# A decoder layer on one core: the expert weight ring with a third slot for six passes only, six embedding products inside the expert passes, x1 kept in DRAM

## The reference

```python
h = rms_norm(x, g_mix); proj = h @ w_in            # conv value | conv gate | q | k | v
conv_out = conformer_conv(c_val, c_gate, ...)      # GLU, causal depthwise conv of 31, LayerNorm, silu
attn = moba_attention(rope(q), rope(k), v)         # 8 heads x 64, blocks of 256, top-3 past blocks + own
x = x + concat(rms_norm(conv_out), rms_norm(attn)) @ w_out          # this x is "x1"
x = x + hier_moe(rms_norm(x, g_ffn), ...)          # top-1 of 4 groups, then top-2 of 8 SwiGLU experts
gate = sigmoid(rms_norm(x, g_ple) @ w_ple_gate + b_ple_gate)
x = x + (p @ w_ple_proj) * gate                    # p: 256 numbers per token, "embedding product"
out = rms_norm(x, g_final)
```

## Time and profile before

| | us |
|---|---|
| median of 3 runs | 597.26 |
| lowest, highest | 595.72, 597.45 |
| the profiled execution's own time | 595.68 |
| its span | 593.8 |

### The profile page before, as it was taken

How to read it: one execution, slowest core, us unless ns; L and a number is a source line. 1 busy time by engine, 2 the same in 40 slices (tenths; PEclk the granted TensorE clock), 3 DMA queues, 4 the chain that set the end, 5 groups by cost and what they waited for, 6 DMA issues and landing times.

```text
span 593.8 us, 8744 instructions
## 1 busy us (share of the span) xinstructions
PE 506.3 (85%) x3193; PEld 299.7 (50%) x3193; DVE 295.0 (50%) x559; ACT 185.4 (31%) x355; POOL 77.9 (13%) x91
## 2 busy tenths in 40 slices
PE   1899999998879989945999989787777988899994
PEld 1688888775556668842433323222222332237883
DVE  2509989999996955484122121101111111167676
ACT  4832320325785352512011010000000000056655
POOL 0570000000032040010211111111110111000000
PEclk9999999999799989975999998888899888999998
DMA  8920400444505050594699999999999899748003
GB/s 336 387 77 2 146 11 8 155 155 161 216 1 214 1 214 35 187 415 167 257 416 421 417 419 422 418 411 419 400 396 420 357 395 413 313 185 331 1 1 141
DMA packets 34741, 146.10 MB, mean 246 GB/s; under 512 B 5776, under 2 KB 6032, under 8 KB 22928
## 3 DMA queue, kind: packets, MB, share of 16 engines
q1 hardware_dynamic: 28800, 133.72, 56.6%
q0 software_dynamic: 5328, 10.50, 4.7%
q10 hardware_dynamic: 576, 1.37, 0.6%
HBM read 140.85 MB, written 12.58 MB: 258 GB/s over the span
## 4 chain that ended last, share of the span: by engine, by line
PE 50%; SPq 20%; DMA 12%; DVE 8%; ACT 5%; issue 4%; POOL 1%; DVEq 0%; POOLq 0%; ACTq 0%
PE bank L1466 15%; SPq L563 9%; DMA wring<-w_up_in 8%; PE bank L1706 8%; PE bank L1770 7%; PE bank L1566 5%; SPq L570 4%; SPq L496 4%; PE bank L1490 4%; DMA wring<-w_in_in 2%; PE bank L1726 2%; PE bank L1749 2%; DMA arena<-rows_d,tfirst 1%; PE bank L1607 1%; DVE wring L1072 1%
## 5 line engine op out<-in xcount | busy, mean ns | idle before, releaser
L1706 PE MATMUL bank<-wring,arena 128*32 128x512 f32 x704 | 90.0, 670 | 20.3 <-DMA wring<-w_up_in 18.0
L1010 DVE SCALAR_TENSOR_TENSOR mix<-arena,pr,mix 128x512 f32<-128x512 f32 x120 | 86.6, 790 | 0.0
L1362 DVE TENSOR_TENSOR arena<-arena,bank 128x256 f32<-128x256 f32 x16 | 6.7, 421 | 141.7 <-ACT arena L898 141.7
L1706 PEld LDWEIGHTS bank<-wring,arena 128*32 128x32 f32 x704 | 27.5, 121 | 81.7 <-issue 76.9
L898 ACT ACTIVATE arena<-bank 128x256 f32<-128x256 f32 x16 | 6.2, 384 | 145.1 <-PE bank L1706 145.1
L1706 PE MATMUL bank<-mix,arena 128*32 128x512 f32 x240 | 40.4, 663 | 7.9 <-DMA arena<-w_up_in 7.9
L1726 PE MATMUL bank<-wring,arena 128*32 128x512 f32 x352 | 40.0, 595 | 5.3 <-ACT arena L901 5.3
L1706 PE MATMUL bank<-arena 128*32 128x512 f32 x80 | 40.3, 663 | 0.0
L1367 DVE COPY arena<-bank 128x512 f32<-128x512 f32 x16 | 11.1, 692 | 53.4 <-PE bank L1726 53.4
L1466 PE MATMUL bank<-hT_hi,win_hi 128*128 128x512 f32 x128 | 33.5, 398 | 1.9 <-DVE hT_lo L988 1.3
L1466 PE MATMUL bank<-hT_lo,win_hi 128*128 128x512 f32 x128 | 31.6, 389 | 0.0
(11 more groups left out here) (258 smaller groups left out, 901.4 us busy)
## 6 DMA issues: line engine op xcount, KB each, us to landing
wring<-w_gate_in SPq DMA_DIRECT2D x22, 1024.0 KB, 15.5
wring<-w_up_in SPq DMA_DIRECT2D x22, 1024.0 KB, 18.8
wring<-w_down_in SPq DMA_DIRECT2D x22, 1024.0 KB, 20.8
wring<-w_in_in SPq DMA_DIRECT2D x5, 2048.0 KB, 19.3
arena<-w_down_in SPq DMA_DIRECT2D x5, 1024.0 KB, 11.6
mix<-w_gate_in SPq DMA_DIRECT2D x5, 1024.0 KB, 15.1
mix<-w_up_in SPq DMA_DIRECT2D x5, 1024.0 KB, 17.2
arena<-w_gate_in SPq DMA_DIRECT2D x5, 1024.0 KB, 19.2
```

The lines of the kernel that those rows point to most:

```text
L1010: ins = dve.scalar_tensor_tensor(out=mixc[:, mm, :], in0=u[:, mm, j:j + S], scalar=w, in1=mixc[:, mm, :], op0=ALU.mult, op1=ALU.add)
L1706: ins = pe.matmul(pb[2 + s][lo:hi, :], xgT[:, s, k, lo:hi], up_w(w, a)[:, :, k, :], start=(k == 0), stop=(k == DK - 1))
```

## The change

1. *Start.* SP issues the constant tables and the router weights, behind the four chunks of w_in. ACT issues only the identity (64 KB) and the parameters. eps is set by a DVE memset, and ACT runs one square root on it first. PE waits for the identity; the waits for the tables move to their first uses.
2. *Ring.* Slot 2 is used by passes 2 and 5 only. Passes 6 to 15 alternate between slots 0 and 1, so the last pass is in slot 1. `last` is n - 3 up to pass 7 and n - 2 from pass 8. Between the reloads of passes 7 and 8 SP loads w_pp and pT into the arena, once pass 5 is done.
3. *x1.* SP stores `xs` tile by tile to a DRAM tensor `x1_d` after the output projection, and reads it back behind the weights of pass 15. In between, `xs` holds the gate and up weights of pass 3, a = 0 (2.1 MB), issued ahead of the passes.
4. *Rows first.* The up DMAs of pass 2, a = 1, and all that SP issues behind them, wait until the first two gathers have landed.
5. *Embedding products.* Six of the eight stand at the head of passes 8 to 13, in banks 4 and 5, each with its copy on ACT. Two stay in the tail.
6. *Tail.* w_pg's first half goes to slot 0 once pass 14 is done; bias and final gain are issued right behind it instead of behind the y tiles and the second half. The y tiles go to slot 1. DVE adds one y tile at a time between the splits.

The same addresses move with slots 0 and 1 (`wpg`, `yg`, `x2_lo` and the rest). The core of the diff:

```diff
+THREE = 2 * SLOTS
+MADE = 8
...
-            return n % SLOTS if n < STRAIGHT else (STRAIGHT % SLOTS, (STRAIGHT + 1) % SLOTS)[n % 2]
+            return n % SLOTS if n < THREE else n % 2
...
+        def load_of(n):
+            return n // SLOTS + 1 if n < THREE else n // 2
+        def aside(n, a):
+            return isinstance(n, int) and n == SLOTS and a == 0
+        def up_aside():
+            return xs[:].rearrange("p t n -> p (t n)").rearrange("p (w k n) -> p w k n", w=2, k=DK)
...
@@ sync
+            sp.dma_start(c[:, P:C_MASK], cst[:, P:C_MASK]).then_inc(const_loaded, 16)
+            sp.dma_start(c[:, C_MASK:C_END], cst[:, C_MASK:C_END]).then_inc(const_loaded, 16)
+            sp.dma_start(wr[:], w_r.rearrange("(p k) n -> p k n", k=DK)).then_inc(wr_loaded, 16)
...
+            for t in range(TT - 1):
+                for half in range(2):
+                    banks.wait_emptied(sp, ("outc", 2 * t + half))
+                sp.dma_start(x1_rows[:, t], xs[:, t, :]).then_inc(x1_stored, 16)
             banks.wait_full(sp, ("outc", 2 * TT - 1))
             load_up(1, 1, 1)
             for a in range(2):
                 load_down(1, 1, a)
-            for a in range(2):
-                load_up(2, 2, a)
+            for half in range(2):
+                banks.wait_emptied(sp, ("outc", 2 * TT - 2 + half))
+            sp.dma_start(x1_rows[:, TT - 1], xs[:, TT - 1, :]).then_inc(x1_stored, 16)
+            load_up(2, 2, 0)
+            for s in range(2):
+                sp.wait_ge(gathered[s], 16)
+            load_up(2, 2, 1)
...
+            for i, src in enumerate((w_gate, w_up)):
+                sp.dma_start(up_aside()[:, i],
+                             src[bass.ds(expert(SLOTS, 0), 1)].rearrange("e (p k) n -> p (e k) n", k=DK)
+                             ).then_inc(aside_loaded, 16)
+            for n in range(SLOTS, THREE + 2):
+                reload(n, slot_of(n), n - SLOTS)
+            sp.wait_ge(up_done, THREE)
+            sp.wait_ge(down_done, THREE)
+            sp.dma_start(wpp, w_pp.rearrange("(p k) n -> p k n", k=PK)).then_inc(ple_loaded, 16)
+            sp.dma_start(pTs, pT.rearrange("(p k) n -> p k n", k=PK)).then_inc(ple_loaded, 16)
+            with sp.Fori(THREE // 2 + 1, STRAIGHT // 2) as i:
+                for s in range(2):
+                    reload(2 * i + s, s, 2 * i + s - 2)
...
-            sp.wait_ge(down_done, STRAIGHT)
-            sp.dma_start(wpp, w_pp.rearrange("(p k) n -> p k n", k=PK)).then_inc(ple_loaded, 16)
-            sp.dma_start(pTs, pT.rearrange("(p k) n -> p k n", k=PK)).then_inc(ple_loaded, 16)
+            sp.dma_start(xs[:], x1_rows).then_inc(x1_loaded, 16)
+            sp.wait_ge(down_done, 2 * last_pair + 1)
             sp.dma_start(wpg[0], pg[:, :, 0:512]).then_inc(pg_loaded[0], 16)
+            sp.dma_start(brow, b_pg.rearrange("a n -> (a n)").partition_broadcast(P)).then_inc(bias_loaded, 16)
+            sp.dma_start(gfin, g_final.partition_broadcast(P)).then_inc(last_loaded, 16)
...
+            banks.wait_full(sp, ("ple", 2 * TT - 1))
             sp.dma_start(wpg[1], pg[:, :, 512:D]).then_inc(pg_loaded[1], 16)
...
@@ scalar
-            act.dma_start(c[:, 0:C_MASK], cst[:, 0:C_MASK]).then_inc(const_loaded, 16)
-            act.dma_start(c[:, C_MASK:C_END], cst[:, C_MASK:C_END]).then_inc(const_loaded, 16)
+            act.dma_start(c[:, 0:P], cst[:, 0:P]).then_inc(ident_loaded, 16)
             act.dma_start(pr[:], prm).then_inc(prm_loaded, 16)
-            act.dma_start(wr[:], w_r.rearrange("(p k) n -> p k n", k=DK)).then_inc(prm_loaded, 16)
+            act.wait_ge(eps_set, 1)
+            act.activation(unused[:], eps[:], ACT.Sqrt)
...
+                if isinstance(n, int) and MADE <= n < STRAIGHT:
+                    ple_out(n - MADE)
...
@@ vector
+            dve.wait_ge(x1_loaded, 16)
...
@@ tensor, one(n, ...)
+                if isinstance(n, int) and MADE <= n < STRAIGHT:
+                    pe.wait_ge(hidT_ready, n)
+                    if n == MADE:
+                        pe.wait_ge(ple_loaded, 32)
+                    ple(n - MADE)
                 pe.wait_ge(xgT_ready, 2 * (n + 1))
                 wait(pe, hid_ready, n - 1)
-                pe.wait_ge(up_loaded[w], 64 * loads)
+                pe.wait_ge(up_loaded[w], 64 * loads - (32 if w == 0 and not (isinstance(n, int) and n < SLOTS) else 0))
+                if aside(n, 0):
+                    pe.wait_ge(aside_loaded, 32)
...
-            for q in range(2 * TT):
+            for q in range(STRAIGHT - MADE, 2 * TT):
                 ple(q)
```

More of the change, by code:

```diff
@@ L91 @@
 C_NUM = C_COL + 2
[L92 to L93 removed]
+C_END = C_NUM + 4 * TT
 PM = TAPS + 4
```

130 lines of the change are left out of this document (76 added, 54 removed).

## The result

| | us |
|---|---|
| before, median of 20 runs | 597.65 (595.71 to 599.26) |
| after, median of 20 runs | 593.72 (591.62 to 598.16) |
| ratio, 95% interval | 0.9944 (0.9927 to 0.996) |
| profiled execution of after | 592.78, span 590.6, mean granted clock 0.946 |
| forecast | 590.7 |

The change makes the kernel 0.56% faster, 3.3 us by the ratio and 2.9 by the two profiled executions (595.68 to 592.78). The forecast was 6.6. The direction was right; about half of the gain did not come. The trace says in which stretch.

A forecast was written before the change was run, and what follows sets the result against it. Bounds taken: transfers at the head, the first gather before the passes, full DMA from 286, then the y-row trip. Sum: -3.2 - 3.2 - 5.5 + 4.3 - 1.5 + 0.4 + 2.1 = -6.6, giving 590.7 us, range 586 to 594.

The forecast's parts named there:

- Head, -3.2: Start: with tables and router weights out of the way, w_in's first chunk lands earlier, saving 3.2 us.
- rival 4: Start: hT_hi on ScalarE, not the chunk, is last, so the head gains nothing; 593.9 us, chance 0.10.
- First gather, -3.2: Before the expert passes: with SP's weights held back, the gather takes 5.0 us instead of 8.17, saving 3.2 us.
- Set aside, -5.5: Expert stream: half of pass 3's ups loaded early lets pass 4's ups land after 11.0 us instead of 16.5.
- two short holes: Expert stream: gaps until the first pass's down product and until the second's up product are done.
- rival 2: The gather stays at 8 us and pass 3's early half only moves a hole; 599.4, half 595.1; chance 0.17.
- w_pp and pT inside, +4.3: Expert stream: their 1.57 MB between pass 7's and pass 8's weights costs 4.3 us, 3.7 at the least.
- Two slots, -1.5: Passes 8 to 13: two slots feed PE as fast as three; five passes slightly shorter, saving 1.5 us.
- rival 3: From pass 8 the two-slot loop is too short, a pass takes 19.4 us; 609.8 us, chance 0.11.
- Embedding products inside, 0: Passes 8 to 13: six products fit PE's waits for weights and cost nothing; leaving the tail gains nothing.
- Tail, +0.4 and +2.1: After pass 15: first gate product 0.4 us later; PE idles, and its clock at half costs 2.1 us.
- Rival 1: Tail gains: early sums, clock holds, first gate product at about +25 after pass 15's ups; 582.8 us, chance 0.10.

The follow-up runs named there:

- run 2: Kernel before with only the start changed: tables and router weights behind the four chunks, eps from a memset, one early square root; 0.9948 of before.
- run 3: Changed kernel without SP's wait for the first two gathers; 0.9996 of before.
- run 1: Changed kernel with nothing set aside: all of pass 3's up weights come through the ring; 0.9972 of before, median 596.76 us.
- run 5: Changed kernel with all eight embedding products in the tail, in two banks, their data still loaded between passes 7 and 8; 1.002 of before.
- run 8: Changed kernel with the third slot kept to pass 8, four embedding products inside the passes and four in the tail; 0.9912 of before.
- Run 4: Changed kernel with pass 5's up weights (a = 0) set aside instead of pass 3's; 0.9903 of before, median 593.13 us.
- run 6: Changed kernel with all eight embedding products in the tail in two banks, and w_pp and pT loaded behind pass 15's weights; 1.002 of before.
- run 7: Changed kernel with all eight embedding products in the tail, in four banks; 0.9981 of before.
- run 10: Changed kernel with DVE's tail order of before, both y tiles added before the split of the tile ahead; 0.9909 of before, median 591.55 us.
- run 9: Changed kernel with bias and final gain loaded behind the y tiles and w_pg's second half; 0.9943 of before.

## Why the prediction was right or wrong

- **Head, -3.2: right in mechanism.** Measured -3.1 (run 2), in an interval that can't tell it from 1.6; in after 2.3 are left at the end of the projections. The chunk stayed last, so rival 4 fell.
- **First gather, -3.2: right.** Measured -3.1 (run 3), with 4.84 us against 5.0 from issue to landing.
- **Set aside, -5.5: the step that failed.** Measured -1.7 in time (-2.9 by the medians) and -2.3 to -2.9 in the trace (run 1). The prediction said that the stream "has two short holes" and "becomes dense with pass 4's ups, which find it empty", landing after 11.0 us. The holes were named and not priced: in after they took 3 us of traffic, and pass 4's ups, issued 10 us behind pass 3's down weights, took 14.2. Nor was the landing of pass 4's ups the right place to read the gain: in runs 5 and 8 the same load landed after 11.2 us, as forecast, and the distances were still 232.3 and 233.4. Its bounds went down to 0 for just this reason; I took the far end instead of working out the bytes that SP could issue between 280 and 294. Run 4 moves the same 2.1 MB to a pass at which SP issues without such holes, and the stretch shrinks to the forecast's length in its trace; the time gained is 2.4 us by the ratio and 0.8 by the medians. So the size of the step is measured, and the holes as its cause are supported, not proved. That is rival 2 in half of its form: "pass 3's early half only moves a hole".
- **w_pp and pT inside, +4.3: right.** 3.6 to 3.9 at pass 15, 4.3 at the place where they lie (runs 5 and 6); two single traces don't tell these apart.
- **Two slots, -1.5: not shown.** Both the slots of before and the two of after give 16.6 us a pass over passes 10 to 15, and over passes 8 to 13 at most 1.4 us can be seen; rival 3's loop didn't bind (run 8). The forecast compared the last passes of before with its middle ones and took the difference for an effect of the slot.
- **Embedding products inside, 0: wrong in the tail, right in the passes.** Leaving them behind pass 15 costs 2.2 us by the times (run 7), of which the trace shows 1.3; the forecast's "the 10.5 us of products that leave the tail are worth nothing there" was too low by that.
- **Tail, +0.4 and +2.1: 1.9 measured, with some luck.** The y trip is right to 0.2 us at each stage. The start of the gate product is 1.4 late instead of 0.4, nearly all of it the order of the sums (run 10: 1.3). The slow clock costs 0.5 in after behind that start. In run 10 it cost 1.4 over the first eight products and in run 9 2.0 over the first sixteen, near the forecast's 2.1: after had it cheap. Rival 1 asked for early sums and a held clock and got neither.

By time: head -3.1, gather -3.1 and set aside -1.7 make -7.9. The measured whole is -3.3, so the rest (w_pp and pT, slots, tail) is +4.6, where the forecast had +5.3. The miss of 3.3 us is therefore 3.8 from the step of the set-aside weights and 0.2 from the first two, less 0.7. Each price comes from ratios and is known to 1.5 to 2 us; by the medians the three are 3.0, 5.0 and 2.9, and the set-aside step is the one that falls short either way. The traces agree: the passes 0 to 15 are 3.1 longer than forecast. These prices come from runs that each gave or took one part, so what parts do to each other is spread over them; between experiments of different chips I compare by ratio to before.

## What to carry to other kernels

A load that is moved ahead is worth something only if the queue can spend the time it frees: list what the issuing engine waits for next, in its order, and count the bytes that it can still issue until then; take the load of the pass behind those waits, not of the one ahead of them. (The run for it is 2.4 us better by the ratio and 0.8 by the medians, so test it.) Work that runs beside a wait of the same engine is also what keeps that engine's clock up, so before moving it away ask what fills the wait then. And an earlier start at the low clock may gain little (run 9 nothing, run 10 0.4 us in the trace of its tail): try it together with what holds the clock.
